# One-token delta rule of eight samples: states as the moving operand past zero-padded queries and keys

## The chip, the core and the metric

The kernel runs on one core of one Trainium2 chip. The metric is the device time of one launch in microseconds (us). Engines are named as in the profile: PE is TensorE (PEld its weight loads), DVE is VectorE, ACT is ScalarE, POOL is GpSimd, SP is SyncE. The granted clock of PE stands in the profile as a share of 2.4 GHz: 1.00 is 2.4 GHz and 0.50 is 1.2 GHz.

## The reference

The program is one step of a two-layer hybrid decoder for a prompt of 256 tokens and for 8 samples of one token each, all in float32. Layer 0 has a recurrent branch, differential attention and a dense SwiGLU; layer 1 has a gated delta rule and a top-2-of-8 expert SwiGLU. The change touches only the delta rule of the samples. There each sample `b` and head `h` (8 heads) has a state `S` of 128x128, and with one token the chunked form of the reference comes down to

```python
# per sample b and head h; q and k are L2-normed, g = log decay, beta = write strength
eg    = exp(g)
v_new = beta * (v - eg * (k @ S))          # k @ S: 128 numbers
o     = eg * (q @ S) + (q . k) * v_new     # q @ S: 128 numbers
S     = eg * S + outer(k, v_new)           # written back to HBM
```

So `q @ S` and `k @ S` are wanted for 64 states (8 heads by 8 samples), 64 KB each. The outputs `o` are then normed per head, gated and projected.

## The kernel before

It is written engine by engine. Every engine runs its own list of instructions in order; the lists meet through counted semaphores (`sig` raises one, `at` says what to wait for). A wait holds everything that stands behind it in that engine's list. Activations lie with features on the 128 partitions and tokens (256 of the prompt, then 8 samples) along the free axis.

The stage around the change comes after the prompt's chunked delta rule and before the output projection of the odd layer (`w_out_o`), some 633 to 689 us into the span. Its states lie in SBUF: heads 0 to 3 in a lent slot of the weight ring, heads 4 to 7 over the finished q, k and v columns (`s_all[h]`, 128 features by 8 samples by 128), loaded by POOL's queue (L611). On each engine the stage is a loop over the heads:

- PE, per turn `h`: `state_products(h + 1)`, the products of head `h + 1` (L2491: for each of 8 samples the state is the weight, and two columns, q and k, move past it; a float32 matmul is two instructions, so 16 of them); `state_rows(h)`, a transpose of the three-part new value of head `h` (L2503); `state_outer(h - 1)`, two matmuls that make the 8 outer products (L2511); and in turns 2 to 5 two `head_rows` (L2526), which spread the prompt's norm factors over the partitions. Turn 0 has `head_sums` (L2519) besides. Before the loop stand 8 transposes of the keys (L2481) and `state_products(0)`.
- DVE, per turn `h`: `sample_out(h + 1)` (L1870 to L1880: eight small operations that read the products of head `h + 1` from PSUM and make the new value and the output), `sample_outer_in(h)` (L1890), `sample_state(h - 1)` (L1897: adds the outer products to the scaled state), and in turns 2 to 5 two `normed` (L1909).
- ACT, per turn `h`: eight scalings of the states of head `h` by their decays, in place (L1290), after it has waited for the products of that head; then the wait for `sample_state(h - 1)` and the issue of its write to HBM (L1310). Turns 1, 6 and 7 have parts of the norm between these two (L1294, L1283, L1299 to L1305).

Three orders matter for what follows. `sample_out(h + 1)` waits for the products of head `h + 1` alone. The products of head `h` wait for `s_o` of head `h - 2`, because two PSUM banks take turns. And ACT's scaling of head `h` stands behind its wait for the state of head `h - 2`. After the loop ACT squares the samples' outputs (L1299), PE sums them (L2542, L2543), ACT and DVE finish the norm, and the projection begins (L963).

Of the kernel before, what the change touches and what calls it, by code (L numbers as in the profile page):

```python
# [10 lines left out]
ACT = mybir.ActivationFunctionType  # L11
# [3 lines left out]
P = 128  # L15
# [8 lines left out]
def program(nc, A, O):  # L24
# [3 lines left out]
    TS = A["x_sample"].shape[0]  # L28
# [16 lines left out]
    _, _, HC, DK, DV = A["state_delta_s"].shape  # L45
    QKV = A["conv_delta_w"].shape[2]
    NQ = QKV // P
# [8 lines left out]
    with ExitStack() as ctx:  # L56
# [15 lines left out]
        def sig(name):  # L72

            if name not in step_at:
                return sem(name)
            engine, first, count = step_at[name]
            assert given.get(engine, 0) == first + given.get(name, 0) and given.get(name, 0) < count, (name, given.get(engine, 0), first)
            given[engine] = given.get(engine, 0) + 1
            given[name] = given.get(name, 0) + 1
            return sem(engine)  # L80

        def at(name, count=1):

            if name not in step_at:
                return sem(name), count
            engine, first, most = step_at[name]
            assert 0 < count <= most, (name, count)
            return sem(engine), first + count
# [79 lines left out]
        ident = sb("ident", [P, P])  # L168
# [15 lines left out]
        work = under("work", [P, W])  # L184
# [6 lines left out]
        bank = [ctx.enter_context(nc.psum_tensor(f"bank{i}", [P, CHUNK_COLS], F32)) for i in range(8)]  # L191
# [165 lines left out]
        def cut(o, *dims):  # L357
            return shaped(work[:, o:o + math.prod(dims)], dims)
# [4 lines left out]
        GRP = NG * P  # L363
        QKV0 = INV0 + KD * T
        TMP0 = QKV0 + NQ * T
        A_0 = HC * T + HC * P
# [50 lines left out]
        s_all = [v.rearrange("p (b e) -> p b e", b=TS) for v in s_place]  # L417
# [43 lines left out]
        R3 = 3 * TS  # L461
# [4 lines left out]
        v_three = cut(A_0 + HC * P + HC * R3, 2, R3)  # L466
        same_row = small[0:R3, 0:TS]
        qkv_s = cut(A_0 + HC * P + HC * R3 + 2 * R3, NQ, TS)
        q_s, k_s, v_s1 = (qkv_s[:, k * HC:(k + 1) * HC, :] for k in range(3))
        vn_s = [vec1(TS) for _ in range(2)]  # L470
        outer_banks = (5, 6)
# [144 lines left out]
        V, SC, PE, GP = nc.vector, nc.scalar, nc.tensor, nc.gpsimd  # L616
# [389 lines left out]
        def _(act_e):  # L1006
# [274 lines left out]
            def o_high(r):  # L1281
                act_e.wait_ge(*at("on_gated", (r + 1) * HALF))
                SC.activation(h_hi[:, r * HALF:(r + 1) * HALF, 0:TP], oT[:, r * HALF:(r + 1) * HALF, 0:TP], ACT.Copy).then_inc(sig(f"on_hi{r}"), 1)  # L1283

            for h in range(HC + 1):
                if h < HC:
                    act_e.wait_ge(*at("s_egb", 1))
                    act_e.wait_ge(*at("s_ks", h + 1))
                    for b in range(TS):
                        last = SC.activation(s_all[h][:, b, :], s_all[h][:, b, :], ACT.Copy, scale=egb[:, 0, h, b:b + 1])  # L1290
                    last.then_inc(sig("s_scaled"), 1)
                if h == 1:
                    act_e.wait_ge(*at("on_ss", 1))
                    SC.activation(o_prompt_r, bank[0][0:HC, 0:TP], ACT.Sqrt, bias=eps_q[0:HC, :], scale=1.0 / DV).then_inc(sig("on_root"), 1)  # L1294
                if h == HC - 2:
                    o_high(0)
                if h == HC - 1:
                    act_e.wait_ge(*at("s_o", HC))
                    SC.activation(o_sample_sq, oT[:, :, TP:T], ACT.Square).then_inc(sig("on_sample_sq"), 1)  # L1299
                    act_e.wait_ge(*at("on_sample_ss", 1))  # L1300
                    SC.activation(o_sample_sq, bank[2][:, 0:HC * TS].rearrange("p (h b) -> p h b", h=HC), ACT.Sqrt, bias=eps_q[:], scale=1.0 / DV)\
                      .then_inc(sig("on_sample_root"), 1)
                    o_high(1)
                    act_e.wait_ge(*at("on_done", 1))
                    SC.activation(h_hi[:, :, TP:T], oT[:, :, TP:T], ACT.Copy).then_inc(sig("on_sample_hi"), 1)  # L1305
                if not h:
                    continue
                h -= 1
                act_e.wait_ge(*at("s_state", h + 1))
                q.dma_start(O["delta_s_sample"][0, :, h].rearrange("b d e -> d b e"), s_all[h]).then_inc(sig(f"states{h // NLENT}_written"), 16)  # L1310
# [92 lines left out]
        def _(dve):  # L1403
# [61 lines left out]
            for t in range(NL):  # L1465
                last = V.tensor_scalar(gate_a[:, t, :], gate_a[:, t, :], sp8[:, t:t + 1], None, ALU.mult)
# [17 lines left out]
            for i in range(2 * HB):  # L1484
                g = r_gq if i < HB else r_gk
                dve.wait_ge(*at("qk_b" if i < HB else "qk_b_keys", i % HB + 1))
                last = V.scalar_tensor_tensor(proj[:, Q_ + i, :], proj[:, Q_ + i, :], par[:, g:g + 1], bank[(i + 4) % 8][:, 0:T],
                                              ALU.mult, ALU.mult)
# [17 lines left out]
            for b in range(TS):  # L1506
# [4 lines left out]
                for g in range(NP_):  # L1511
                    last = V.tensor_tensor(kv_mul[:, g, :], pages_kv[:, b % 4, g, :], bank[4 + b % 2][:, :], ALU.mult)
                link(last)
                for g in range(NP_):
                    last = V.reduce_sum(sc_s[:, g, :, :, b].rearrange("p i h -> p h i"),
                                        kv_mul[:, g, :].rearrange("p (h i d) -> p h i d", i=2, d=DH), X)
# [14 lines left out]
            for h in range(HB):  # L1531
                for s, (c0, c1) in enumerate(seg):
                    r = s * HH + 2 * h
                    last = V.tensor_scalar(sc_p[:, 2 * h, c0:c1], sc_p[:, 2 * h, c0:c1], rsum[:, r:r + 1], None, ALU.mult)
# [312 lines left out]
            dve.wait_ge(*at("d_out", 2 * TT))  # L1847
            dve.wait_ge(*at("d_state", 2 * TT))
            prod = inv[:, 0, 0:HC * TS].rearrange("p (h b) -> p h b", h=HC)
            V.tensor_copy(q_s, qT[:, :, TP:T])  # L1850
            V.tensor_copy(v_s1, vT[:, :, TP:T])
            V.tensor_tensor(k_s, kT[:, :, TP:T], r_sample, ALU.mult).then_inc(sig("s_qkv"), 1)
            dve.wait_ge(*at("s_qkv", 1))
            V.tensor_tensor(prod, q_s, k_s, ALU.mult).then_inc(sig("s_prod"), 1)
            behind(dense_lo, dve, "w_in_o", NQC - 1, 1)
            link(V.tensor_copy(k_three[:, :, 0:TS].bitcast(F32R), k_s))
# [6 lines left out]
            def sample_out(h):  # L1863

                eg, be = egb[:, 0, h, :], egb[:, 1, h, :]
                vn = vn_s[h % 2]
                dve.wait_ge(*at("s_ks", h + 1))
                qS = bank[2 + h % 2][:, 0:2 * TS].rearrange("p (b k) -> p b k", k=2)[:, :, 0]
                kS = bank[2 + h % 2][:, 0:2 * TS].rearrange("p (b k) -> p b k", k=2)[:, :, 1]
                link(V.tensor_tensor(vn, kS, eg, ALU.mult))  # L1870
                link(V.tensor_tensor(vn, v_s1[:, h, :], vn, ALU.subtract))
                link(V.tensor_tensor(vn, vn, be, ALU.mult))
                if h >= 2:
                    dve.wait_ge(*at("s_vt", h - 1))
                v3 = v_three[:, h % 2, :]
                link(V.tensor_copy(v3[:, 0:2 * TS].rearrange("p (k b) -> p k b", k=2).bitcast(F32R), vn.unsqueeze(1).broadcast_to([P, 2, TS])))
                V.tensor_tensor(v3[:, 2 * TS:R3].bitcast(F32R), vn, v3[:, 0:TS], ALU.subtract).then_inc(sig("s_v"), 1)
                V.tensor_tensor(vn_t, qS, eg, ALU.mult)
                link(V.tensor_tensor(prod[:, 0, :], vn, qks[:, h, :], ALU.mult))
                V.tensor_tensor(oT[:, h, TP:T], prod[:, 0, :], vn_t, ALU.add).then_inc(sig("s_o"), 1)  # L1880

            def sample_outer_in(h):

# [203 lines left out]
        def _(pe):  # L2087
# [396 lines left out]
            def state_products(h):  # L2484

                pe.wait_ge(*at("s_qkv", 1))
                pe.wait_ge(*at(f"state{h % NLENT}_loaded", 16 * (h // NLENT + 1)))
                if h >= 2:
                    pe.wait_ge(*at("s_o", h - 1))
                for b in range(TS):  # L2490
                    last = PE.matmul(bank[2 + h % 2][:, 2 * b:2 * b + 2], s_all[h][:, b, :],  # L2491
                                     qkv_s[:, h:h + HC + 1:HC, b], start=True, stop=True)
                last.then_inc(sig("s_ks"), 1)

            def state_rows(h):

                pe.wait_ge(*at("s_v", h + 1))
                if h >= 2:
                    pe.wait_ge(*at("s_vd", h - 1))
                else:  # L2500
                    pe.wait_ge(*at("s_krows", h + 1))
                vt = bank[(4, 7)[h % 2]]
                PE.transpose(vt[0:R3, 0:P], v_three[:, h % 2, :], ident[:]).then_inc(sig("s_vt"), 1)  # L2503
# [23 lines left out]
                  .then_inc(sig("on_b"), 1)  # L2527

            state_products(0)
            for h in range(HC):  # L2530
                if h + 1 < HC:
                    state_products(h + 1)
                state_rows(h)
                if h:
                    state_outer(h - 1)
                if h == 0:
                    head_sums()
                if 2 <= h <= 5:
                    head_rows(2 * (h - 2))
                    head_rows(2 * (h - 2) + 1)  # L2540
# [216 lines left out]
```

## Time and profile before

| what | value |
| --- | --- |
| median of three runs | 1756.63 us (1753.97 to 1757.15) |
| profiled execution | 1756.62 us |
| its span | 1754.9 us |
| PE busy in the span | 1675.1 us (95%) |
| DVE busy | 1328.7 us (76%) |
| ACT busy | 1064.4 us (61%) |
| DMA, HBM read and written | 437.28 MB and 7.29 MB, 253 GB/s |
| chain that ended last | PE 84%, DVE 8%, ACT 3% |

The span is the time between the first and the last instruction of the profile; 1.7 us of the execution lie outside it. Most of the span (from 727 us on) is the expert stage. Matmuls are pipelined, so a busy PE need not be a fast PE: the granted clock has to be read beside it. Times of single rows are microseconds from the start of the span, then the duration.

### The profile page before, as it was taken

The page shows a single profiled execution, that of the slowest core. Times are in us where ns is not written, and L with a number is a line of the kernel's source. Part 1 is how long each engine was busy: PE and PEld are TensorE (multiplying, and loading weights), DVE is VectorE, ACT ScalarE, POOL GpSimd, SP SyncE. Part 2 cuts the span into 40 slices and gives each one's busy share as a digit, 9 for nine tenths or more (in the row PEclk, how much of TensorE's full clock was granted, in tenths as well). Part 3 has the DMA queues.
Part 4 walks back from the last instruction along what each step waited for, and adds up shares of the span by engine and source line. Part 5 has one row for each costly group of instructions (what it writes and reads, how often), then busy time and mean ns, then how long its engine had stood idle before and what let it go on. Part 6 is the DMA issues. An engine that isn't in the chain of part 4 may idle for free.

```text
span 1754.9 us, 25078 instructions
## 1 busy us (share of the span) xinstructions
PE 1675.1 (95%) x9513; PEld 1433.1 (82%) x9513; DVE 1328.7 (76%) x1443; ACT 1064.4 (61%) x1054; POOL 188.7 (11%) x234
## 2 busy tenths in 40 slices
PE   7979999999899988999999999999999999999996
PEld 7835999999879967888888888888888888888885
DVE  6883554556776745588898898888887998988985
ACT  5542543435752343677777777776776776776673
POOL 5020211003264601100000000000000000000000
PEclk9968999999999975999999999999999999999999
DMA  9542454653430026499899899899899899999992
GB/s 299 182 148 59 151 188 142 216 177 119 144 105 1 1 74 203 142 360 377 317 359 374 308 367 377 305 370 377 305 367 368 315 366 332 348 368 329 346 374 94
DMA packets 199194, 445.47 MB, mean 254 GB/s; under 512 B 9569, under 2 KB 20995, under 8 KB 199071
## 3 DMA queue, kind: packets, MB, share of 16 engines
q1 hardware_dynamic: 184698, 423.88, 67.1%
q0 software_dynamic: 3968, 12.85, 2.5%
q10 hardware_dynamic: 10448, 7.65, 1.5%
q8 instruction: 54, 0.88, 0.2%
q14 instruction: 26, 0.21, 0.0%
HBM read 437.28 MB, written 7.29 MB: 253 GB/s over the span
## 4 chain that ended last, share of the span: by engine, by line
PE 84%; DVE 8%; ACT 3%; issue 2%; PEld 2%; POOL 1%; DMA 0%; PEldq 0%; ACTq 0%; DVEq 0%; POOLq 0%
PE bank L2645 17%; PE bank L2624 12%; PE bank L2625 12%; PE bank L2629 12%; PE bank L963 5%; PE bank L967 5%; PE bank L976 5%; PE bank L2595 2%; DVE weight_lo L554 1%; ACT weight_hi L551 1%; PE bank L2425 1%; PE bank L2605 1%; PE bank L2491 1%; PE bank L2435 1%; PE bank L2438 1%
## 5 line engine op out<-in xcount | busy, mean ns | idle before, releaser
L554 DVE TENSOR_TENSOR weight_lo<-weight_ring,weight_hi 128x2048 fp32r<-128x2048 f32 (+1 forms) x352 | 797.2, 2274 | 234.3 <-ACT weight_hi L551 218.2
L551 ACT ACTIVATE weight_hi<-weight_ring 128x2048 fp32r<-128x2048 f32 (+1 forms) x358 | 680.2, 1903 | 304.6 <-PE bank L976 98.3
L2624 PE MATMUL bank<-weight_hi,h_lo 128*128 128x512 f32 x896 | 354.2, 395 | 0.1
L2625 PE MATMUL bank<-weight_hi,h_hi 128*128 128x512 f32 x896 | 349.2, 390 | 0.0
L2629 PE MATMUL bank<-weight_lo,h_hi 128*128 128x512 f32 x896 | 239.8, 389 | 0.0
L2629 PEld LDWEIGHTS bank<-weight_lo,h_hi 128*128 128x128 f32 x896 | 168.2, 188 | 35.0
L2624 PEld LDWEIGHTS bank<-weight_hi,h_lo 128*128 128x128 f32 x896 | 168.3, 188 | 34.6 <-DVE h_lo L1999 0.4
L2625 PEld LDWEIGHTS bank<-weight_hi,h_hi 128*128 128x128 f32 x896 | 168.4, 188 | 33.4
L2645 PE MATMUL bank<-weight_hi,h_lo 128*128 128x512 f32 x448 | 120.6, 391 | 1.8 <-DVE h_lo L2004 1.8
L2645 PE MATMUL bank<-weight_hi,h_hi 128*128 128x512 f32 x448 | 119.8, 389 | 0.0
L2645 PE MATMUL bank<-weight_lo,h_hi 128*128 128x512 f32 x448 | 119.8, 389 | 0.0
L554 DVE TENSOR_TENSOR weight_lo<-work,weight_hi 128x2048 fp32r<-128x2048 f32 x48 | 109.8, 2288 | 12.5 <-ACT weight_hi L551 12.5
L963 PE MATMUL bank<-n_hi,weight_hi 128*128 128x264 f32 x608 | 103.3, 292 | 8.9 <-issue 4.5
L551 ACT ACTIVATE weight_hi<-work 128x2048 fp32r<-128x2048 f32 x48 | 92.1, 1920 | 26.4 <-PE bank L2629 20.1
L967 PE MATMUL bank<-n_hi,weight_lo 128*128 128x264 f32 x608 | 100.6, 288 | 5.0 <-POOL weight_lo L607 5.0
L2645 PEld LDWEIGHTS bank<-weight_hi,h_lo 128*128 128x128 f32 x448 | 83.5, 188 | 19.0 <-DVE h_lo L2004 2.1
L2645 PEld LDWEIGHTS bank<-weight_hi,h_hi 128*128 128x128 f32 x448 | 84.1, 188 | 17.6
L2645 PEld LDWEIGHTS bank<-weight_lo,h_hi 128*128 128x128 f32 x448 | 84.1, 188 | 17.5
L963 PEld LDWEIGHTS bank<-n_hi,weight_hi 128*128 128x128 f32 x608 | 85.6, 192 | 13.4 <-issue 10.7
L963 PE MATMUL bank<-h_hi,weight_hi 128*128 128x264 f32 x464 | 87.6, 294 | 4.0 <-DVE work L1451 1.8
L967 PEld LDWEIGHTS bank<-n_hi,weight_lo 128*128 128x128 f32 x608 | 85.7, 192 | 5.4 <-POOL weight_lo L607 5.4
L967 PE MATMUL bank<-h_hi,weight_lo 128*128 128x264 f32 x464 | 85.4, 289 | 0.7 <-DVE weight_lo L554 0.7
(514 smaller groups left out, 2159.9 us busy)
## 6 DMA issues: line engine op xcount, KB each, us to landing
weight_ring<-in_moe_wg SPq DMA_DIRECT2D x104, 1024.0 KB, 7.2
weight_ring<-in_moe_wu SPq DMA_DIRECT2D x96, 1024.0 KB, 7.3
weight_ring<-in_moe_wd SPq DMA_DIRECT2D x88, 1024.0 KB, 6.6
work<-in_moe_wd SPq DMA_DIRECT2D x24, 1024.0 KB, 7.1
weight_ring<-in_w_in_o SPq DMA_DIRECT2D x8, 2048.0 KB, 8.6
work<-in_moe_wu SPq DMA_DIRECT2D x16, 1024.0 KB, 6.3
weight_ring<-in_ffn_wg SPq DMA_DIRECT2D x5, 2048.0 KB, 7.7
weight_ring<-in_ffn_wu SPq DMA_DIRECT2D x5, 2048.0 KB, 8.5
```

Of the source, the lines that this page charges most:

```text
L551: return SC.activation(whi[:, p % SPLIT, 0:size], src, ACT.Copy).then_inc(sig("hi_done"), 1)
L554: V.tensor_tensor(wlo[:, p % SPLIT, 0:size], src, whi[:, p % SPLIT, 0:size].bitcast(F32), ALU.subtract)\
L963: PE.matmul(out, hi[:, jj, cols_], a_hi[:, j0 + j, :], start=first and j == 0, stop=False)
L967: PE.matmul(out, lo[:, jj, cols_], a_hi[:, j0 + part * half + jj, :], start=False, stop=False)
L976: last = PE.matmul(out, hi[:, jj, cols_], a_lo[:, j0 + j, :], start=False, stop=last_one and j == k - 1)
L2425: last = PE.matmul(bank[STREAM[u]][:, k * P:(k + 1) * P], Am[:, h, :], Tt[:, h, :], start=True, stop=True)
L2435: last = PE.matmul(bank[STREAM[u]][:, k * P:(k + 1) * P], Tm[:, h, :], Yb[:, h, :], start=True, stop=True)
L2595: last = PE.matmul(bank[(7, 3)[r]][:, jj * CAP:(jj + 1) * CAP], h_tok[:, i, j * P:(j + 1) * P], sel[:, i, :], start=i == 0, stop=i == NTT - 1)
L2624: PE.matmul(out, hte_l[:, j, :], hi[:, jj, :], start=j == 0, stop=False)
L2625: PE.matmul(out, hte_h[:, j, :], hi[:, jj, :], start=False, stop=False)
L2629: last = PE.matmul(out, hte_h[:, j, :], lo[:, jj, :], start=False, stop=j == KD - 1)
L2645: last = PE.matmul(bank[5 + hf][:, :], lhs[:, c % 2, k, :], rhs[:, kk, hf * CHUNK_COLS:(hf + 1) * CHUNK_COLS], start=c == 0 and k == 0 and ...
```

## The change

The roles of the operands in the sample products are swapped. Queries and keys of a head become weights, the states move. For each sample a block of 16 columns is built that is zero but for column `b` (its q) and column `8 + b` (its k). The matmul of sample `b` then gives a row `b` with `q @ S` and a row `8 + b` with `k @ S` and adds zeros to the other rows, so that eight matmuls in a row accumulate 16 rows of 128 in one PSUM bank. ACT copies the rows to SBUF (`take_rows`), PE transposes them to columns (`state_columns`), and DVE reads the columns as before, though q's eight and k's eight now lie together.

DVE clears the two column buffers once (`memset`) and places q and k of a head with two strided copies (`place_columns`): heads 0 and 1 before the loop, head `h + 2` at the end of `sample_out(h)`. In ACT's list `take_rows(0)` comes before the loop and `take_rows(h + 1)` behind the scalings of head `h`; the scalings no longer wait for the products by themselves. In PE's list `state_columns(h + 1)` stands between `state_rows(h)` and `state_outer(h - 1)`.

```diff
+            take_rows(0)
             for h in range(HC + 1):
                 if h < HC:
                     act_e.wait_ge(*at("s_egb", 1))
-                    act_e.wait_ge(*at("s_ks", h + 1))
                     for b in range(TS):
                         last = SC.activation(s_all[h][:, b, :], s_all[h][:, b, :], ACT.Copy, scale=egb[:, 0, h, b:b + 1])
                     last.then_inc(sig("s_scaled"), 1)
+                if h + 1 < HC:
+                    take_rows(h + 1)
...
+            def take_rows(h):
+                act_e.wait_ge(*at("s_rows", h + 1))
+                SC.activation(qk_rows[h % 2], bank[2 + h % 2][0:2 * TS, P:2 * P], ACT.Copy).then_inc(sig("s_rows_out"), 1)
...
+            V.memset(qk_cols[0], 0.0)
+            V.memset(qk_cols[1], 0.0)
...
+            def place_columns(h):
+                step = 2 * TS + 1
+                V.tensor_copy(qk_cols[h % 2][:, 0:step * (TS - 1) + 1:step], q_s[:, h, :])
+                V.tensor_copy(qk_cols[h % 2][:, TS:TS + step * (TS - 1) + 1:step], k_s[:, h, :]).then_inc(sig("s_placed"), 1)
...
-                qS = bank[2 + h % 2][:, 0:2 * TS].rearrange("p (b k) -> p b k", k=2)[:, :, 0]
-                kS = bank[2 + h % 2][:, 0:2 * TS].rearrange("p (b k) -> p b k", k=2)[:, :, 1]
+                qS = bank[2 + h % 2][:, 0:TS]
+                kS = bank[2 + h % 2][:, TS:2 * TS]
...
+                if h + 2 < HC:
+                    place_columns(h + 2)
...
+                pe.wait_ge(*at("s_placed", h + 1))
                 for b in range(TS):
-                    last = PE.matmul(bank[2 + h % 2][:, 2 * b:2 * b + 2], s_all[h][:, b, :],
-                                     qkv_s[:, h:h + HC + 1:HC, b], start=True, stop=True)
-                last.then_inc(sig("s_ks"), 1)
+                    last = PE.matmul(bank[2 + h % 2][0:2 * TS, P:2 * P], qk_cols[h % 2][:, 2 * TS * b:2 * TS * (b + 1)], s_all[h][:, b, :],
+                                     start=b == 0, stop=b == TS - 1)
+                last.then_inc(sig("s_rows"), 1)
+
+            def state_columns(h):
+                pe.wait_ge(*at("s_rows_out", h + 1))
+                PE.transpose(bank[2 + h % 2][:, 0:2 * TS], qk_rows[h % 2], ident[0:2 * TS, 0:2 * TS]).then_inc(sig("s_ks"), 1)
...
             state_products(0)
+            state_columns(0)
             for h in range(HC):
                 if h + 1 < HC:
                     state_products(h + 1)
                 state_rows(h)
+                if h + 1 < HC:
+                    state_columns(h + 1)
                 if h:
                     state_outer(h - 1)
```

## Rows read from the trace of the kernel before

**Rows 1.** Page, granted clock of PE in 40 equal slices, tenths of full speed

```profile
PEclk9968999999999975999999999999999999999999
```

**Rows 2.** Windows of the stage: length, busy time (instructions), granted clock, DMA share, GB/s

```profile
core 0: us, PE busy (x) PEld busy (x) DVE busy (x) ACT busy (x) POOL busy (x), PEclk, DMA share, GB/s
667.00:674.00 7.00, 7.00 (x26) 5.62 (x25) 4.65 (x15) 2.44 (x8) 1.42 (x2) 0.50 0.30 78
690.00:700.00 10.00, 10.00 (x66) 10.00 (x66) 1.82 (x11) 1.92 (x1) 0.00 (x0) 0.76 0.45 131
```

**Rows 3.** Timeline, PE's matmuls of one turn: start, duration, engine, line, operation, count

```profile
672.43 1.21 PE L2511 MATMUL bank<-n_lo_odd 24*128 24x512 f32 x2
673.45 1.90 PE L2526 MATMUL bank<-work,ident 8*128 8x256 f32 x4
675.28 3.57 PE L2491 MATMUL bank<-work 128*128 128x2 f32 x16
```

**Rows 4.** Timeline, DVE's and ACT's part of the same turn

```profile
672.31 0.17 DVE L1870 TENSOR_TENSOR sm<-bank,sm 128x8 f32<-128x8 f32 x1 [1.95 <-PE bank L2491]
673.21 0.16 DVE L1878 TENSOR_TENSOR sm<-bank,sm 128x8 f32<-128x8 f32 x1
673.28 0.16 DVE L1879 TENSOR_TENSOR work<-sm 128x8 f32<-128x8 f32 x1
673.75 1.21 DVE L1890 TENSOR_TENSOR n_lo_odd<-small,bank 24x1024 fp32r<-24x1024 f32 x1
674.89 1.26 DVE L1897 TENSOR_TENSOR work<-work,bank 128x512 f32<-128x512 f32 x2
676.19 0.38 ACTq L1310 DMA_DIRECT2D out_delta_s_sample<-work  x1
676.67 2.44 ACT L1290 ACTIVATE work<-work,sm 128x128 f32<-128x128 f32 x8 [4.14 <-DVE work L1897]
679.02 1.04 ACT L1283 ACTIVATE h_hi<-hT 128x1024 fp32r<-128x1024 f32 x1
```

**Rows 5.** Timeline, first operation of `sample_out` for heads 2, 3, 4 and 7

```profile
648.15 0.17 DVE L1870 TENSOR_TENSOR sm<-bank,sm 128x8 f32<-128x8 f32 x1 [5.25 <-PE bank L2491]
653.40 0.09 DVE L1870 TENSOR_TENSOR sm<-bank,sm 128x8 f32<-128x8 f32 x1
659.13 0.17 DVE L1870 TENSOR_TENSOR sm<-bank,sm 128x8 f32<-128x8 f32 x1 [1.38 <-PE bank L2491]
678.89 0.17 DVE L1870 TENSOR_TENSOR sm<-bank,sm 128x8 f32<-128x8 f32 x1 [1.95 <-PE bank L2491]
```

**Rows 6.** Timeline, the nearest rows to the added operations, and DVE's wait before the loop

```profile
628.98 0.20 ACT L1273 ACTIVATE sm<-bank 128x64 f32<-128x64 f32 x1
629.10 2.29 DVE L554 TENSOR_TENSOR weight_lo<-weight_ring,weight_hi 128x2048 fp32r<-128x2048 f32 x1 [3.48 <-ACT weight_hi L551]
...
631.92 1.88 PE L2481 MATMUL bank<-ident,work 128*24 128x128 f32 x8 [5.81 <-DVE work L1858]
632.98 0.59 ACT L1279 ACTIVATE n_lo_odd<-bank 24x512 fp32r<-24x512 f32 x1 [3.57 <-PE bank L2481]
...
685.61 0.24 ACT L1299 ACTIVATE work<-hT 128x64 f32<-128x64 f32 x1
685.90 0.50 PEld L2542 LDWEIGHTS bank<-work,ones 128*128 128x128 f32 x2 [2.54 <-ACT work L1299]
...
687.06 0.31 ACT L1301 ACTIVATE work<-bank,small 128x64 f32<-128x64 f32 x1 [1.21 <-PE bank L2543]
```

**Rows 7.** Timeline, `head_sums`, and the products of head 2 right behind it

```profile
640.58 5.13 PE L2519 MATMUL bank<-work,sm 128*8 128x256 f32 x16
646.17 1.95 PE L2491 MATMUL bank<-work,weight_ring 128*128 128x2 f32 x16
```

**Rows 8.** Timeline, the output projection: its first matmuls, and four at the raised clock

```profile
689.12 1.25 PE L963 MATMUL bank<-h_hi,weight_hi 128*128 128x264 f32 x4 [0.22 <-ACT h_hi L1305]
695.20 0.64 PE L967 MATMUL bank<-h_hi,weight_lo 128*128 128x264 f32 x4
```

More of the change, by code:

```diff
@@ L468, in program @@
         qkv_s = cut(A_0 + HC * P + HC * R3 + 2 * R3, NQ, TS)
+        QK0 = A_0 + HC * P + HC * R3 + 2 * R3 + NQ * TS
+        qk_cols = [work[:, QK0 + k * 2 * TS * TS:QK0 + (k + 1) * 2 * TS * TS] for k in range(2)]
+        qk_rows = [work[0:2 * TS, QK0 + 4 * TS * TS + k * P:QK0 + 4 * TS * TS + (k + 1) * P] for k in range(2)]
+        assert QK0 + 4 * TS * TS + 2 * P <= A_0 + 4 * GRP
         q_s, k_s, v_s1 = (qkv_s[:, k * HC:(k + 1) * HC, :] for k in range(3))
@@ L1853, in _ @@
             dve.wait_ge(*at("s_qkv", 1))
+            def place_columns(h):
+                step = 2 * TS + 1
+                V.tensor_copy(qk_cols[h % 2][:, 0:step * (TS - 1) + 1:step], q_s[:, h, :])
+                V.tensor_copy(qk_cols[h % 2][:, TS:TS + step * (TS - 1) + 1:step], k_s[:, h, :]).then_inc(sig("s_placed"), 1)
+            place_columns(0)
+            place_columns(1)
             V.tensor_tensor(prod, q_s, k_s, ALU.mult).then_inc(sig("s_prod"), 1)
```

## The prediction

> **What bounds the kernel now.** I first read the page's row of granted clocks [rows 1]: behind the first 180 us PE has its full clock nearly everywhere, but for the 15th and 16th slice (of 43.9 us each, so 614 to 702 us), where the changed stage lies. Next the windows [rows 2]: from 667 to 674 us PE is busy for 7.00 of 7.00 us, at a clock of 0.50, while DVE is busy for 4.65 and ACT for 2.44. So PE's list sets the end here. The timeline confirms it [rows 3, 4]: `sample_out` starts at 672.31 us with an idle time of 1.95 us ended by the products (L2491), and the next one at 678.89 [rows 5], so a turn takes 6.58 us. Most of it is the products (3.57 us for 16 instructions, some 0.22 each), then `head_rows` (1.90) and the outer products (1.21); the ends overlap. DVE and ACT wait in every turn.
>
> Early turns are different: between heads 2 and 3 `sample_out` moves from 648.15 to 653.40 (5.25 us), between 3 and 4 by 5.73, then three times by 6.59 on average, 19.76 us in all [rows 5]. From head 7's `sample_out` at 678.89 to the first matmul of the projection at 689.12 [rows 8] it is 10.23 us.
>
> PE's clock has a story of its own. Behind `head_sums`, which began at 640.58, the 16 products of head 2 took 1.95 us [rows 7] against 3.57 later [rows 3]: the same instructions at 2.4 and at 1.2 GHz.
>
> **The change part by part.** *PE's products.* 16 instructions of 128 moving columns with 16 weight columns take the place of 16 with two moving columns and 128 weight columns. The nearest row is L2481: eight instructions of 128 moving columns with 24 weight columns take 1.88 us at half clock, at most 0.24 each and about (1.88 - 0.2)/7 = 0.24 without the last one's end [rows 6]. 16 of them are 3.4 to 3.8 us against 3.57 now. At the same clock the swap takes nothing out of PE. What it can bring is the clock.
>
> *The new hand-over.* Per head ACT copies 16x128 out of PSUM and PE transposes it. The copy lies between 0.20 (128x64) and 0.59 us (24x512) [rows 6]; on the line between the two, 128 elements are 0.26. For the transpose I take the path from ACT to PE to ACT after the loop: ACT's square begins at 685.61 and takes 0.24, the next ACT operation starts at 687.06, 1.21 us later, with four PE instructions of 128 weight columns between (L2542, L2543) [rows 6]. Less three at 0.22, one instruction with both hand-overs takes 0.55; at full clock about 0.35. Together 0.8 us per head.
>
> *Where it stands.* This decides. `take_rows(h + 1)` stands in ACT's list behind the scalings of head `h`, those stand behind the issue of head `h - 2`'s write, and that waits for `sample_state(h - 2)` on DVE. `sample_out(h + 1)` on DVE now waits for the transposed rows, so for ACT; `sample_outer_in(h)` and `sample_state(h - 1)` stand behind it, and the next issue on ACT waits for that state. It is a ring with one turn per head. Before, ACT's scalings were in no such ring, since DVE got the products from PE alone. Its length from rows of one turn [rows 4]:
> - `sample_out`, L1870 to L1890: 673.75 - 672.31 = 1.44
> - two placement copies: starts of independent operations of this size lie 0.07 to 0.08 apart (L1878, L1879), so 0.16 (0.32 at full durations)
> - `sample_outer_in`, L1890 to L1897: 1.14
> - `sample_state` and the hand-over, L1897 to the issue: 1.30
> - issue to the first scaling: 0.48
> - eight scalings, first start to the next ACT operation, L1290 to L1283: 2.35
> - copy of the rows: 0.26
> - transpose with its hand-overs: 0.55
>
> The sum is 7.68 us, 7.5 at full clock, and 7.52 behind head 6, where nothing is left to place. PE fits inside at half clock: behind the transpose it has the outer products, `head_rows` and the next products, 1.2 + 1.9 + 3.6 = 6.7 us at most, against the 6.9 that pass until ACT takes the rows (7.68 - 0.26 - 0.55). So the ring sets the turn: 1.1 us more than PE's 6.58.
>
> *The start.* Memsets and four placements come on DVE before 629.10, where it idles 3.48 us for ACT [rows 6]; at 0.2 us each (128x64 copies and less) they are hidden, and cost up to 1.2 us without that cover. PE now stops between the products of heads 0 and 1 for copy and transpose, 0.8 us, and again behind head 1. Against this the clock may rise earlier. In the trace of before it was up by the time of L2491 at 646.17, and it was down again in the turn at 667 us. How long PE works before it rises: `head_sums` started at 640.58 and its 16 took 5.13 us, where 16 at 0.43 would be 6.9 and at 0.21 3.4, so it rose about 3 us in [rows 7]; at the projection the rows are at half clock from 689.12 and at full before 695.20, so up to 6 us [rows 8]. From 631.92, where PE starts, that gives a rise between 635 and 638 us if the new products act like these. Then the products of head 1 and `head_sums` run at full clock, and head 2's `sample_out` comes at some 647.0 us, 1.2 before 648.15. If the clock rises as late as now, the two stops push it to 649.2, 1.1 later. I take 0.9 earlier.
>
> *The sum.* Head 2: -0.9. Heads 2 to 3: 7.68 - 5.25 = +2.4. Heads 3 to 4: 7.68 - 5.73 = +1.95. Heads 4 to 7: 7.68 + 7.68 + 7.52 - 19.76 = +3.1. Two turns with a transpose at full clock: -0.4. Together +6.2 us. The last 10.23 us keep their chain (head 7's `sample_out`, state 5, issue, scalings, norm), and the work behind it, the projection and the experts, moves as a whole. The profiled execution, 1756.62 us (1754.9 of it the span), agrees with the median of 1756.63, so the forecast is 1762.8 us.
>
> *The clock rule.* Rows first: from 667 to 674 us PE's record is busy all the time and the clock is 0.50 [rows 2]. The Trainium skill (TensorE: Matmul & The Clock Gate, Part 1) says the throttled state is the default, and that activity, how busy PE has recently been, releases it. By the busy record alone this stage would be at full clock already and the swap could bring nothing; the trace does not agree with it in that wording, so I let the clock be open in the next part.
>
> **The rivals.** *The clock stays up, into the projection.* The projection's first four take 1.25 and later ones 0.64 [rows 8]; the window from 690 to 700 us has a mean clock of 0.76 [rows 2], so about 4.8 of its 10 us are at half, with the 0.9 before it 5.7 us. At full clock they are 2.9, 2.8 us saved, and 1760.0. Against it: once the ring sets the turn PE is idle for one to four us in each, and the last products are some 10 us before the projection.
>
> *The clock rises late.* The stops break up the start, head 2 comes 1.1 us later instead of 0.9 earlier, and no turn has the faster transpose: +6.2 + 2.0 + 0.4 = +8.6, 1765.2. With the copies at 0.59 and the placement at 0.32 (ends of their bounds) the ring is 8.17, five turns of it 2.3 more, 1767.5.
>
> *Faster: ACT is not in the ring.* If the rows were ready on ACT early enough, PE's clock would decide, and at full clock the turn would be DVE's work: 1.44 + 0.16 + 1.14 + 1.30 and two `normed`, about 0.85, so 4.9 us. Heads 2 to 7 then take 24.5 instead of 30.7 us, and head 2 comes 0.9 earlier: 1749.5. It decides from the point at which the ring falls under 6.58, that is, if 1.1 of its 7.68 us are not there. What speaks for it is that PE's clock is the only bound seen now; against it stands the order of ACT's list, in which nothing can overtake the scalings, and that seven eighths of the ring are measured rows.
>
> **How the numbers follow.** Forecast, the ring with an early rise: 0.70, some 1761 to 1764.5. Late rise or long copies: 0.14. Clock up to the end: 0.08. ACT not in the ring: 0.08. A measurement of this kernel can tell about 0.2% (3.5 us) from no change. The clock case lies on that border, half of it counts as no change; a little of the faster one as well. So slower 0.88, same 0.05, faster 0.07. The range reaches from 1758.5 (the clock case with its uncertainty) to 1767.5 (the long copies) and leaves out the faster rival.
>
> **What would show it.** In the changed trace `sample_out`'s idle time should be ended by the transpose, the transpose's by ACT's copy, and that copy should start right behind the eight scalings in each turn from head 3 on, with turns of 7.4 to 7.8 us. PE should show idle time in these turns whatever its clock, and L1310 should come at once when the state is done. Head 2's `sample_out` at 647 us would show the early clock, at 649 the late one. The forecast is wrong if the copy of the rows ever waits for PE in the later turns (then PE's clock still decides), or if turns come under 6.6 us.

## The result and the profile after

The changed kernel took 1762.95 us (median of 7 runs) against 1757.15 us for the kernel before (7 runs on the same chip): a ratio of 1.0031 [1.0021, 1.0041], 3.7 to 7.2 us slower. One of the 7 runs, at 5782.69 us, lies far outside the others (1760.31 to 1763.44) and is left out of the ratio. Forecast were 1762.8 us and "slower". Two later comparisons of the same two kernels gave 1.0014 [1.0005, 1.0023] and 1.0016 [1.0007, 1.0025]. All three intervals lie above 1, but the size is uncertain: 0.1 to 0.3%, with the 0.2% that a measurement can tell in the middle.

The profiled execution of after took 1762.95 us, 1761.2 of it the span. Page of after, the granted clock in 40 slices, the counterpart of [rows 1]:

```profile
PEclk9968999999999986999999999999999999999998
```

The 15th and 16th slice rose from 7 and 5 tenths to 8 and 6; but for the last one all others are as before. The changed stage has more clock and takes longer all the same.

Timeline of after, first operation of `sample_out` (now L1890) for heads 2, 3, 4 and 7, and the first matmuls of the projection; these answer [rows 5] and [rows 8]. Columns are start, duration, engine, line, operation, and in brackets the idle time before it and what ended it:

```profile
647.01 0.17 DVE L1890 TENSOR_TENSOR sm<-bank,sm 128x8 f32<-128x8 f32 x1 [3.91 <-PE bank L2520]
654.20 0.17 DVE L1890 TENSOR_TENSOR sm<-bank,sm 128x8 f32<-128x8 f32 x1 [1.74 <-PE bank L2520]
661.38 0.17 DVE L1890 TENSOR_TENSOR sm<-bank,sm 128x8 f32<-128x8 f32 x1 [2.60 <-PE bank L2520]
...
682.85 0.17 DVE L1890 TENSOR_TENSOR sm<-bank,sm 128x8 f32<-128x8 f32 x1 [2.65 <-PE bank L2520]
...
692.87 1.25 PE L967 MATMUL bank<-h_hi,weight_hi 128*128 128x264 f32 x4 [0.28 <-ACT h_hi L1315]
```

Head 2 comes 1.14 us earlier than before; then every turn is 7.1 to 7.2 us long, while before it was 5.25, 5.73 and three times 6.59. The projection starts 3.75 us later (692.87 against 689.12). Each idle time of DVE is now ended by the new transpose (L2520).

Timeline of after, the products and the copy that lead up to a turn, and then this whole turn in the order of its ring, the counterpart of [rows 3] and [rows 4]:

```profile
662.70 1.92 PE L2514 MATMUL bank<-work 128*16 128x128 f32 x16
...
667.98 0.25 ACT L1291 ACTIVATE work<-bank 16x128 f32<-16x128 f32 x1
...
668.60 0.17 DVE L1890 TENSOR_TENSOR sm<-bank,sm 128x8 f32<-128x8 f32 x1 [2.65 <-PE bank L2520]
...
669.85 0.17 DVE L1869 COPY work<-work 128x8 f32<-128x8 f32 x1
669.92 0.17 DVE L1870 COPY work<-work 128x8 f32<-128x8 f32 x1
670.00 1.20 DVE L1912 TENSOR_TENSOR n_lo_odd<-small,bank 24x1024 fp32r<-24x1024 f32 x1
671.13 1.27 DVE L1919 TENSOR_TENSOR weight_ring<-weight_ring,bank 128x512 f32<-128x512 f32 x2
...
671.25 3.54 PE L2514 MATMUL bank<-work 128*16 128x128 f32 x16
...
672.43 0.38 ACTq L1320 DMA_DIRECT2D out_delta_s_sample<-weight_ring  x1
672.85 2.44 ACT L1298 ACTIVATE work<-work,sm 128x128 f32<-128x128 f32 x8 [4.62 <-DVE weight_ring L1919]
...
675.20 0.25 ACT L1291 ACTIVATE work<-bank 16x128 f32<-16x128 f32 x1
...
675.51 0.23 PE L2520 MATMUL bank<-ident,work 16*128 16x16 f32 x1 [0.51 <-ACT work L1291]
...
675.77 0.17 DVE L1890 TENSOR_TENSOR sm<-bank,sm 128x8 f32<-128x8 f32 x1 [2.60 <-PE bank L2520]
```

The products that the copy at 667.98 takes had ended at 664.62, with PE at 2.4 GHz, and ACT had nothing to do until its issue at 665.20; the copy comes 3.4 us after them, right behind the eight scalings. In the turn shown whole the products run at 1.2 GHz and end at 674.79, and the copy stands right behind the scalings again, 2.35 us from their start. The order of ACT's list decides, not the data. (The Trainium skill, PSUM — Partial Sum Buffer, Engine vs sequencer instructions, calls ScalarE's queue strictly first in, first out; the rows agree.)

Chain of waits of after in this stretch, some of its longer pieces (start, duration, what); it walks round the ring once, and the products are not in it:

```profile
668.28 0.29 PE bank L2520
669.21 0.19 DVE work L1896
670.09 1.11 DVE n_lo_odd L1912
671.20 1.21 DVE weight_ring L1919 x2
672.43 0.38 ACTq L1320
672.85 2.44 ACT work L1298 x8
675.51 0.24 PE bank L2520
```

Waits of after from 656 to 686 us (engine, line, what it waited for: total, times, longest). Both PE and DVE wait for ACT's copy or for what hangs on it; before, DVE's line here was a wait for the products:

```profile
DVE sm L1890 <- PE bank L2520: 10.5, 4, 2.6
...
PE bank L2520 <- ACT work L1291: 6.7, 4, 3.5
```

Windows of after (length, busy time and instructions of PE, PEld, DVE, ACT, POOL, granted clock, DMA share, GB/s), to be read beside [rows 2]:

```profile
650.00:654.00 4.00, 0.07 (x1) 0.07 (x1) 2.46 (x3) 2.60 (x9) 0.00 (x0) 1.00 0.46 131
661.00:665.00 4.00, 3.72 (x24) 2.66 (x24) 3.45 (x13) 0.06 (x1) 0.00 (x0) 1.00 0.00 0
668.00:672.00 4.00, 3.72 (x11) 2.49 (x12) 3.23 (x13) 0.23 (x2) 0.00 (x0) 0.50 0.00 0
```

In the first stretch PE is idle for all but 0.07 of 4 us. The other two are about the same part of two turns: in one PE has 2.4 GHz, in the other 1.2, and both turns last 7.2 us. PE's clock no longer decides here.

### The profile page after: what moved, and what is told of

The parts are those of the page before. It is cut to its first block, busy times and chain, and to the rows that moved or that the text cites. A ratio compares the mean times of both kernels' runs of the same rounds, so it can differ in the third digit from the quotient of the medians.

```text
span 1761.2 us, 25118 instructions
## 1 busy us (share of the span) xinstructions
PE 1671.0 (95%) x9521; PEld 1423.8 (81%) x9521; DVE 1330.8 (76%) x1461; ACT 1066.0 (61%) x1062; POOL 188.8 (11%) x234
## 4 chain that ended last, share of the span: by engine, by line
PE 82%; DVE 9%; ACT 4%; issue 2%; PEld 2%; POOL 1%; DMA 0%; PEldq 0%; ACTq 0%; DVEq 0%; POOLq 0%
PE bank L2675 17%; PE bank L2654 12%; PE bank L2659 12%; PE bank L2655 12%; PE bank L967 5%; PE bank L971 5%; PE bank L980 5%; PE bank L2625 2%; DVE weight_lo L558 1%; ACT weight_hi L555 1%; PE bank L2447 1%; PE bank L2635 1%; PE bank L2457 1%; PE bank L2460 1%; PE bank L2262 1%
```

## Experiments

The kernel before and the changed one were each run two more times as kernels of their own, so that each group of experiments has its own traces of both.

**Both kernels again.** No edit.

> The kernel before, unchanged, for a second trace. The first two traces differ by 6.3 us in span, of which 3.75 lie before the output projection (692.87 against 689.12), 1.3 in the expert stage (a turn of it takes 126.54 against 126.34 us) and the rest at the end, where the clock dipped once. Theory A, these two come from run to run: the expert turn moves by some 0.1 to 0.2 us between two traces of the same kernel, and a dip at the end comes or does not. Theory B, they come from the change (another program, other positions): 126.34 us here again, and no dip, while the changed kernel shows 126.54. The stage itself should repeat to 0.3 us: a turn of 6.58 us, projection some 56 us behind the first sample product.

> The changed kernel, unchanged. Theory A (expert turn and end vary from run to run): the expert turn may come out anywhere between 126.3 and 126.6 us, and the dip at the end need not come again. Theory B (they belong to the change): 126.54 us and the dip again. Ring theory for the stage: turns of 7.1 to 7.3 us, each with the scalings right in front of the copy of the rows; projection 3.5 to 4 us later than before. Time against before: 1.0025 to 1.0040.

> The kernel before, unchanged, a third trace, for what lies behind the stage. So far a turn of the expert loop took 126.34 us in one trace of it and 126.54 in the other, and the stretch from the last of these turns to the end 149.84 and 148.15. Theory A (these come and go from run to run): either value again, the two not tied to a kernel. Theory B (126.54 belongs to the changed kernel): 126.34. From the first transpose of the stage to the projection: 57.2 to 57.4 us.

> The changed kernel, unchanged, a third trace and more times. Both of its traces had expert turns of 126.54 us and a stretch of 151 us at the end, some 2 us more than before in all. Theory A: 126.34 comes up here too, or the end is shorter. Theory B: 126.54 and 151 again. From the first transpose to the projection 60.7 us. With the stage alone (3.4 us) the ratio is 1.0019; with theory B it is 1.003.

The kernel before against itself: 0.9995 [0.9986, 1.0004] and 0.9998 [0.9989, 1.0007]. From the first key transpose to the projection it took 57.20, 57.41 and 56.86 us in three traces, mean 57.16; the changed kernel 60.69, 60.69 and 60.77. So the stage is 3.5 us longer, and 3.3 to 3.9 whichever two traces are taken. What lies behind it varies in both kernels: one turn of the experts takes 126.34 or 126.54 us (before: 126.34, 126.54, 126.54; after: 126.54, 126.54, 126.34), and the part from the last of these turns to the end 148.2 to 151.3 us. Part of that is the clock in the last microseconds. Window of the first trace of after:

```profile
1741.00:1744.00 3.00, 3.00 (x11) 2.33 (x10) 0.00 (x0) 0.00 (x0) 0.00 (x0) 0.67 0.00 0
```

The same window of its third trace:

```profile
1741.00:1744.00 3.00, 3.00 (x14) 2.17 (x12) 0.00 (x0) 0.00 (x0) 0.00 (x0) 1.00 0.00 0
```

The first profiled difference, 6.3 us of span, is thus 3.75 from the stage and 2.5 from places where the two kernels are the same. The latter come and go in both kernels, and nothing ties them to the change.

**The rows taken ahead of the scalings.** One block moved in ACT's list of the changed kernel.

```diff
             for h in range(HC + 1):
+                if h + 1 < HC:
+                    take_rows(h + 1)
                 if h < HC:
                     ... eight scalings ...
-                if h + 1 < HC:
-                    take_rows(h + 1)
```

> The changed kernel with one edit: in ACT's list the copy of the rows of head h+1 stands ahead of the scalings of head h, not behind them. Nothing is left out. Ring theory (the turn is set by state, issue, eight scalings, copy, transpose, sample_out, outer, state): the eight scalings (2.35 us) and the issue fall out of the way of the rows, so that a turn takes 4.7 to 5.5 us at full clock (DVE's own work, 4.7) and up to 6.6 at half clock (PE's), projection 5 to 9 us earlier than before, time 1748 to 1753 us or 0.995 to 0.998. Rival (the hand-over itself costs, a copy and a transpose on PE's way in each turn): turns stay at 7.1 to 7.3 and the time at 1.003.

It took 1750.30 us, ratio 0.9972 [0.9961, 0.9983]; the stage takes 51.49 us, turns 4.96 to 5.50. Timeline: the copy of the rows now waits for a state (in the turns to heads 3, 5 and 7) or for the products (heads 4 and 6), and behind copy and transpose DVE waits at most 0.46 us where it waited 2.6:

```profile
656.65 0.27 ACT L1291 ACTIVATE work<-bank 16x128 f32<-16x128 f32 x1 [2.94 <-PE bank L2514]
...
657.30 0.17 DVE L1890 TENSOR_TENSOR sm<-bank,sm 128x8 f32<-128x8 f32 x1 [0.46 <-PE bank L2520]
```

Without the scalings the ring has 2.35 us less and the turns are shorter by 1.7 to 2.2. The ring is still closed, only shorter. Timeline of this kernel, the steps of one turn from a state to the next:

```profile
660.13 1.27 DVE L1919 TENSOR_TENSOR weight_ring<-weight_ring,bank 128x512 f32<-128x512 f32 x2
...
661.43 0.38 ACTq L1320 DMA_DIRECT2D out_delta_s_sample<-weight_ring  x1
661.85 0.27 ACT L1291 ACTIVATE work<-bank 16x128 f32<-16x128 f32 x1 [2.60 <-DVE weight_ring L1919]
...
662.17 0.23 PE L2520 MATMUL bank<-ident,work 16*128 16x16 f32 x1 [1.26 <-ACT work L1291]
...
662.45 0.17 DVE L1890 TENSOR_TENSOR sm<-bank,sm 128x8 f32<-128x8 f32 x1 [0.27 <-PE bank L2520]
...
665.46 1.27 DVE L1919 TENSOR_TENSOR weight_ring<-weight_ring,bank 128x512 f32<-128x512 f32 x2
```

It is 5.33 us, and the chain of waits of this kernel goes this way, through issue, copy and transpose but not through the scalings. DVE waits for the transpose in only 0.27 of it.

**The write one turn later.** Here the ring is made to close over two turns instead of one: ACT waits in turn `h` for the state of head `h - 2`, not `h - 1`, so that the scalings no longer stand behind a state that hangs on this turn's copy.

```diff
-            for h in range(HC + 1):
+            for h in range(HC + 2):
...
-                if not h:
+                if h < 2:
                     continue
-                h -= 1
+                h -= 2
                 act_e.wait_ge(*at("s_state", h + 1))
```

> The changed kernel with another edit: ACT issues the write of a head's state one turn later (head h-2 in turn h instead of h-1), the copy of the rows stays behind the scalings. Nothing is left out. Ring theory: the ring then closes over two turns, 7.2 / 2 = 3.6 us per turn, and falls under the work of DVE (4.7) and of PE, so turns of 4.7 to 6.6 us and a time of 0.995 to 0.999. Rival (copy and transpose as such, or the scalings in front of the copy as such, cost the time, whatever the wait): turns stay at 7.1 to 7.3 and the time at 1.003.

1748.95 us, ratio 0.9964 [0.9951, 0.9978]: turns of 4.83 to 5.39, stage 50.78 us. Waits of this kernel from 650 to 676 us:

```profile
DVE sm L1890 <- PE bank L2520: 0.4, 1, 0.4
```

A window of it:

```profile
659.00:666.00 7.00, 5.33 (x36) 3.66 (x34) 6.83 (x19) 2.98 (x10) 1.41 (x2) 1.00 0.26 75
```

DVE waits 0.4 us for the transpose in all, where after has 9.6 in the same stretch, and it is busy for 6.83 of 7 us: its own work is the bound in this stretch, with PE at 2.4 GHz.

**Both edits.**

> The changed kernel with both edits, the copy of the rows ahead of the scalings and the write one turn later. Nothing is left out. Ring theory: with either edit the ring is gone already, and the turns are set by DVE (4.7) and by PE at whichever clock it has (3.5 to 6.5), so little more is gained: turns of 4.7 to 5.3 us, ratio 0.9955 to 0.997. Rival (each edit takes off its own part of the ring): 0.993 to 0.995.

1750.17 us, ratio 0.9966 [0.9952, 0.9979], stage 50.85 us: no more than with either edit alone, as expected. That with either edit the ring is gone, as I wrote there, holds for the late write, whose ring closes over two turns; with the rows ahead of the scalings alone it is shorter, and near enough to DVE's own work that nothing more can be told from the times.

**The late write again.**

> The changed kernel with the late write, unchanged from its first run, for a second set of times. Stage 50.8 us (6.4 under before), ratio 0.996 to 0.997, expert turns of either value.

1749.56 us, ratio 0.9968 [0.9957, 0.9979], so the gain repeats. Its trace doesn't: from head 4's `sample_out` on the turns last 6.91 us, and the stage 55.96. Window of this trace:

```profile
659.00:666.00 7.00, 6.96 (x27) 4.29 (x25) 4.96 (x17) 2.71 (x9) 1.41 (x2) 0.50 0.26 75
```

Timeline of it:

```profile
661.85 0.27 ACT L1291 ACTIVATE work<-bank 16x128 f32<-16x128 f32 x1 [4.04 <-PE bank L2514]
...
662.29 1.20 PE L2538 MATMUL bank<-n_lo_odd 24*128 24x512 f32 x2
...
665.13 3.60 PE L2514 MATMUL bank<-work 128*16 128x128 f32 x16
```

The same program is here at 1.2 GHz where it had 2.4 in the trace above, and then ACT's copy waits 4.04 us for the products: PE sets the turn, at 6.91 us. That is more than the 6.59 of before: with PE at 1.2 GHz the swap gains nothing in a turn, and what the late write gains there hangs on the clock. The two traces part behind the products of head 4, which take 3.08 us in the first and 2.93 in this one: the next `head_rows` take 1.02 and 1.90 us. What decides between the two was not found.

**Half of the scalings.** Changed kernel; it leaves out four of the eight scalings of each head.

```diff
-                    for b in range(TS):
+                    for b in range(TS // 2):
```

> The changed kernel with four of the eight scalings of each head left out on ACT (the states of samples 4 to 7 are not decayed); all else is there. It takes a known term out of the ring: four scalings are 4 x 0.294 = 1.18 us. Ring theory: from head 3 on a turn falls from 7.18 by 1.2 us to 6.0, as long as PE fits (at half clock it needs some 6.5, so a turn may lie between 6.0 and 6.5); four turns and the end make the span 5 to 6 us shorter than that of the changed kernel. Rival (the turn is set by PE's list with the stop for copy and transpose): turns stay at 7.2, only ACT's idle time grows by 1.2.

The first turns shrink from 7.19 and 7.18 to 6.03 and 6.08 us, 1.16 and 1.10 less, and four scalings are 2.35 / 2 = 1.18. The scalings lie in the ring with their whole length. The later turns stop at 6.91 us, as in the trace just shown, and for the same reason: PE is full at half clock and the copy waits for it. Window of this kernel:

```profile
667.00:674.00 7.00, 6.96 (x26) 4.33 (x25) 4.49 (x14) 1.55 (x5) 1.41 (x2) 0.50 0.34 85
```

Timeline of it:

```profile
671.61 0.27 ACT L1291 ACTIVATE work<-bank 16x128 f32<-16x128 f32 x1 [0.74 <-PE bank L2514]
```

Its one run took 1758.62 us; the stage is 57.32 us long, 3.4 less than in after, where 5 to 6 were expected, since a turn at half clock takes 6.91 us and not 6.5.

**The ring without the swap.** In the kernel before, with its old products, ACT copies the 16 columns out of PSUM behind the scalings, and DVE reads the copy.

```diff
+            def take_columns(h):
+                act_e.wait_ge(*at("s_ks", h + 1))
+                SC.activation(qk_copy[h % 2], bank[2 + h % 2][:, 0:2 * TS], ACT.Copy).then_inc(sig("s_columns_out"), 1)
+            take_columns(0)
...
-                    act_e.wait_ge(*at("s_ks", h + 1))
                     ... eight scalings ...
+                if h + 1 < HC:
+                    take_columns(h + 1)
...
-                dve.wait_ge(*at("s_ks", h + 1))
+                dve.wait_ge(*at("s_columns_out", h + 1))
```

> The kernel before with one part of the change alone: its products as they were (two columns past the state as weight), but ACT copies the 16 columns of the next head from PSUM to SBUF behind the scalings of this head, and DVE reads the copy. No zero-padded weights, no transpose. Nothing is left out. Ring theory: turns of 7.18 less the transpose hand-over (0.27) less the little that the copy of 16 columns is shorter, so 6.8 to 6.9 us from head 3 on against 6.58 (and 5.25 and 5.73 for the first two), with PE at half clock throughout; the time 3 to 5 us above before, 1.0015 to 1.003. Rival (the swapped products, not the ring, cost the time): as before, 6.58, ratio 1.000 to 1.0005.

Its turns are 6.66 us each from head 3 on, where those of before start at 5.25 and 5.73 and end at 6.59; 6.8 to 6.9 were expected. The stage takes 59.76 us, 2.6 more than the mean of before, and 2.3 of it lie in the first two turns. The ratio of 1.0009 [1.0000, 1.0019] is under the 1.0015 to 1.003 expected, and does not tell the ring theory from its rival; the trace does. Timeline of one turn:

```profile
668.48 0.17 DVE L1879 TENSOR_TENSOR sm<-work,sm 128x8 f32<-128x8 f32 x1 [2.22 <-ACT work L1290]
...
669.03 3.57 PE L2500 MATMUL bank<-work 128*128 128x2 f32 x16
...
674.95 0.16 ACT L1290 ACTIVATE work<-bank 128x16 f32<-128x16 f32 x1
675.14 0.17 DVE L1879 TENSOR_TENSOR sm<-work,sm 128x8 f32<-128x8 f32 x1 [2.22 <-ACT work L1290]
```

DVE waits 1.36 us for ACT's copy in the first of these turns and 2.22 in each of the others. The products do not hold it up: those that began at 669.03 ended at 672.60, and the copy comes at 674.95. So in this trace most of the loss is there without any of the new products: 2.6 of 3.5 us. The swap adds the transpose to the ring (0.5 us a turn) and gives back 1.6 us at the start, where head 2 comes 14.83 us after the first key transpose against 16.43 here.

**The late write without the swap.** The edit of the late write, in the kernel before.

> The kernel before with the one edit of the late write alone (ACT issues the write of a head's state one turn later). Nothing is left out. It tells how much of the gain of the late write in the changed kernel (0.9964) belongs to the swap. Theory (PE at half clock sets the turn before, ACT waits anyway): turns stay at 6.58 us; only the way from head 7 to the projection, where the scalings of head 7 stand behind a write, gets shorter, by up to 2 us; ratio 0.999 to 1.000. Rival (the late write is what gains, whatever the products): 5 to 7 us, 0.996 to 0.997.

Ratio 1.0001 [0.9992, 1.0010]; turns 5.24, 5.74 and 6.6, stage 57.14, and its last part 10.22, not shortened. In before the late write opens nothing, since ACT's scalings stand in no ring there. So the 6 us gained above come from the swapped products and the late write together; in the traces the turns are shorter than before where PE has its higher clock.

## Why the prediction was right, and where its terms were off

*The bound moves from PE to a ring over DVE, ACT and PE.* Right, and each sign that was named for it is there but for the length of a turn (7.1 to 7.2 us where 7.4 to 7.8 was named): DVE's idle time is ended by the transpose, the transpose's by the copy, the copy stands right behind the scalings, and the two clocks give the same turn. Either edit to ACT's list takes 1.7 to 2.4 us out of a turn, and half of the scalings 1.1 to 1.2, as long as PE at half clock does not set it.

*The length of the ring.* Forecast 7.68 us, measured 7.17 in the turn shown:

| part | forecast | after |
| --- | --- | --- |
| `sample_out` with the placement (668.60 to 670.00) | 1.44 + 0.16 | 1.40 |
| `sample_outer_in` (to 671.13) | 1.14 | 1.13 |
| state to issue (to 672.43) | 1.30 | 1.30 |
| issue to the first scaling (to 672.85) | 0.48 | 0.42 |
| eight scalings (to 675.20) | 2.35 | 2.35 |
| copy (to 675.45) | 0.26 | 0.25 |
| transpose with both hand-overs (to 675.77) | 0.55 | 0.32 |

The four terms that were read from one turn and that the change leaves as they are met within 0.06 us. The mis-sized ones are the transpose and the placement, 0.43 of the 0.51 us. The transpose was taken from four PE instructions of 128 weight columns with their hand-overs [rows 6], and its 0.55 is for half clock; the forecast had 0.35 for full clock. In the turn shown it ran at full clock (0.23 us) and takes 0.32; in the turn before, at half clock, 0.37. The prediction had two transposes of the five at full clock; there were three. The placement was priced at 0.16 and is 0.15 by itself (669.85 to 670.00), but it adds nothing to the 1.44: the two copies fall into a pause that DVE had there before, while it waited for the outer products (to 673.64 [rows 3]). `sample_outer_in` began 0.47 us behind L1879 [rows 4], and now it begins 0.42 us behind the same operation (at 669.58) with both copies in between.

*The sum.* In the profiled executions: start and head 2 -1.14 (forecast -0.9), heads 2 to 3 +1.94 (+2.4), 3 to 4 +1.45 (+1.95), 4 to 7 21.47 - 19.76 = +1.71 (+3.1), the last part 10.02 against 10.23, -0.21 (unchanged). Together +3.75 where +6.2 was forecast, which included -0.4 for transposes at full clock. The five turns were 2.35 us too long in the sum, 0.5 each, less that 0.4; the start and the last part gave 0.2 each that was not forecast. That the time came out at 1762.95, so near to 1762.8, is partly chance: 2.5 us of the profiled difference lie behind the stage. With the stage's 3.5 us the change costs 0.20%, and the three ratios lie on both sides of it; 0.88 for "slower by over 0.2%" was too sure.

*PE's products and its clock.* 16 products took 3.54 us at 1.2 GHz in the turn shown, inside the 3.4 to 3.8 that the eight key transposes gave [rows 6]. The clock rose before 637.90 us, where the products of head 1 begin, against 635 to 638 forecast. Timeline of after, the products of heads 0 and 1:

```profile
633.99 3.39 PE L2514 MATMUL bank<-weight_ring,work 128*16 128x128 f32 x16
637.90 1.92 PE L2514 MATMUL bank<-weight_ring,work 128*16 128x128 f32 x16
```

What PE has to do behind the transpose at half clock was put at 6.7 us at most. In the late write's second trace, where PE sets the turn, it is 6.44 us, from the outer products at 662.29 to the end of the products at 668.73; the turn of 6.91 is this with copy and transpose. So the sum was right, and PE fitted into the ring as forecast.

*The clock stays up, into the projection:* it didn't. The first four matmuls take 1.25 us as before. *The late rise:* excluded by head 2 at 647.01. *Long copies:* excluded, the copy takes 0.25 us. *Faster, ACT not in the ring:* it was not the case, but its price was about right. With ACT's list edited the turns are 4.8 to 5.5 us (4.9 forecast) as long as PE has its full clock for most of them, and 1749.5 us, 0.996 of before, were forecast where 0.9964 to 0.9972 was measured. What I had named as its condition, that PE is at full clock, stays open: the late write's second trace has it only until head 4.

So the fastest version is the change with an edit to ACT's list, and which of the two the times do not tell; with the late write it is 0.9964 [0.9951, 0.9978] and 0.9968 [0.9957, 0.9979] of the kernel before.

## What to carry to other kernels

When a hand-over through another engine is added, follow that engine's list backwards from the new instruction until you come to a wait: if that wait hangs on something the new instruction releases, a ring has been closed, and where its sum of durations is longer than what any one engine has to do, it is the new turn, however fast the engine becomes that was to be relieved. Take each term from one real turn, and cost only what is new from elsewhere; here the latter carried most of the error. Order alone can shorten a ring (the scalings moved out of it) or let it close over two turns (the write moved back), and that should be tried before a change like this one is given up.

## What the runs showed of the hardware

One program can run a stretch at either clock level from one execution to the next. The two traces of the late write stand at 1.00 and 0.50 from 659 to 666 us, with turns of about 5 and 6.9 us, and its timed runs in the second comparison spread from 1747.7 to 1752.96 us, of which the traced one is the longest. A single trace of such a stage says little of its median.

Small DVE operations with both inputs in SBUF become slower beside POOL. Timeline of the first trace of the late write, where DVE no longer idles while POOL gates (L847):

```profile
661.07 1.41 POOL L847 TENSOR_TENSOR hT<-hT,work 128x256 f32<-128x256 f32 x2 [3.92 <-DVE hT L1931]
661.31 0.15 DVE L1890 TENSOR_TENSOR sm<-bank,sm 128x8 f32<-128x8 f32 x1
661.49 0.33 DVE L1891 TENSOR_TENSOR sm<-work,sm 128x8 f32<-128x8 f32 x1
661.86 0.65 DVE L1892 TENSOR_TENSOR sm<-sm 128x8 f32<-128x8 f32 x1
662.54 0.17 DVE L1896 CAST work<-sm 128x16 fp32r<-128x16 f32 x1
```

L1891 and L1892 take 0.33 and 0.65 us here and 0.17 where POOL rests (in after at 668.80 and 669.00); L1890, which has one input in PSUM, keeps its 0.15. The Trainium skill (SBUF — State Buffer, Who interferes with whom) says that a DVE instruction with two SBUF inputs contends with a GpSimd instruction that reads SBUF, and that one with at most one does not as long as it is outside the 2-port performance modes; these rows agree. It costs some 0.6 us in a turn in which DVE sets the pace.
